# The halved norm between two layers: where its stages, its root and its products lie, and the order of the work around it

## What is computed

```python
h_lat = h_lat + gt_l[:, None, :] * y_lat                 # y_lat = (o * silu(gate)) @ mla_w_out
...
u_lat = rms_norm(h_lat, norm_g[i]) * (1.0 + sc_l[:, None, :]) + sh_l[:, None, :]
proj = u @ w_in                                          # fourier_mix
z, gate = proj[..., :FOURIER_WIDTH], proj[..., FOURIER_WIDTH:]
...
return (y * jax.nn.silu(gate)) @ w_out
```

## Time and profile before

| | us |
|---|---|
| median of 3 runs | 1463.97 |
| lowest and highest | 1463.37, 1466.03 |
| profiled execution, its own time | 1463.78 |
| span of its trace | 1461.9 |
| first-half norm to end of the gate product FG, about | 354 to 397 of the span |

### The profile page before, as it was taken

How to read it: one execution, slowest core, us unless ns; L and a number is a source line. 1 busy time by engine, 2 the same in 40 slices (tenths; PEclk the granted TensorE clock), 3 DMA queues, 4 the chain that set the end, 5 groups by cost and what they waited for, 6 DMA issues and landing times.

```text
span 1461.9 us, 18234 instructions
## 1 busy us (share of the span) xinstructions
PE 1392.6 (95%) x6933; PEld 1152.3 (79%) x6933; DVE 756.2 (52%) x1024; ACT 578.2 (40%) x886; POOL 501.8 (34%) x235
## 2 busy tenths in 40 slices
PE   5899899999899999999999989999999999999998
PEld 2388677778788888877779879878888888888887
DVE  1389788853845536567542443460635435253342
ACT  4233455543533344445643344343334223132231
POOL 1124001135442294411224214214465444444441
PEclk9999999999999999989999889879999999999999
DMA  9686000116231143311222212113333333333322
GB/s 311 195 275 196 20 11 25 30 43 221 72 113 46 43 143 87 101 43 44 61 72 74 59 43 73 56 30 114 92 95 95 94 100 100 90 96 100 100 89 71
DMA packets 204501, 136.18 MB, mean 93 GB/s; under 512 B 7033, under 2 KB 185834, under 8 KB 204442
## 3 DMA queue, kind: packets, MB, share of 16 engines
q1 hardware_dynamic: 204442, 135.37, 30.8%
HBM read 130.64 MB, written 4.72 MB: 93 GB/s over the span
## 4 chain that ended last, share of the span: by engine, by line
PE 81%; DVE 11%; ACT 3%; issue 2%; DMA 1%; SPq 1%; POOL 0%; ACTq 0%; DVEq 0%
PE psum L1868 26%; PE psum L1869 25%; PE psum L1870 25%; DVE neg_max L1410 1%; DMA w_raw<-in_mla_w_in 1%; DVE pt_lo L1403 1%; PE psum L1909 1%; DVE probs L1398 1%; ACT probs L829 1%; PE psum L2262 1%; ACT w_hi L712 1%; DVE u_lo L1498 0%; PE psum L2388 0%; DVE stage L1783 0%; PE psum L1974 0%
## 5 line engine op out<-in xcount | busy, mean ns | idle before, releaser
L602 POOL TENSOR_TENSOR w_lo<-w_raw,w_hi 128x1024 fp32r<-128x1024 f32 x180 | 438.8, 2441 | 770.7 <-ACT w_hi L712 642.8
L1868 PE MATMUL psum<-u_hi,w_hi 128*128 128x512 f32 (+1 forms) x960 | 374.6, 390 | 12.2 <-DVE u_lo L1498 6.3
L1869 PE MATMUL psum<-u_lo,w_hi 128*128 128x512 f32 (+1 forms) x960 | 364.8, 380 | 0.0
L1870 PE MATMUL psum<-u_hi,w_lo 128*128 128x512 f32 (+1 forms) x960 | 364.4, 380 | 0.0
L712 ACT ACTIVATE w_hi<-w_raw 128x1024 fp32r<-128x1024 f32 x180 | 189.2, 1055 | 197.7 <-PE psum L1870 155.7
L1868 PEld LDWEIGHTS psum<-u_hi,w_hi 128*128 128x128 f32 x960 | 184.2, 192 | 52.6 <-issue 8.9
L1870 PEld LDWEIGHTS psum<-u_hi,w_lo 128*128 128x128 f32 x960 | 184.0, 192 | 34.3
L1869 PEld LDWEIGHTS psum<-u_lo,w_hi 128*128 128x128 f32 x960 | 184.4, 192 | 32.9 <-issue 1.7
L1868 PE MATMUL psum<-y_hi,w_hi 128*128 128x512 f32 x416 | 162.4, 390 | 0.0
L1869 PE MATMUL psum<-y_lo,w_hi 128*128 128x512 f32 x416 | 161.9, 389 | 0.0
L1870 PE MATMUL psum<-y_hi,w_lo 128*128 128x512 f32 x416 | 161.8, 389 | 0.0
(11 more groups left out here) (414 smaller groups left out, 2348.0 us busy)
## 6 DMA issues: line engine op xcount, KB each, us to landing
w_raw<-in_w_in SPq DMA_DIRECT2D x52, 512.0 KB, 3.8
w_raw<-in_w_up SPq DMA_DIRECT2D x32, 512.0 KB, 4.0
w_raw<-in_w_down SPq DMA_DIRECT2D x32, 512.0 KB, 3.7
ada_back<-in_w_ada SPq DMA_DIRECT2D x7, 2048.0 KB, 8.6
ada_w<-in_w_ada SPq DMA_DIRECT2D x5, 2048.0 KB, 9.5
w_raw<-in_fno_w_in SPq DMA_DIRECT2D x16, 512.0 KB, 3.9
w_raw<-in_mla_w_in SPq DMA_DIRECT2D x11, 512.0 KB, 8.1
w_raw<-in_mla_w_out SPq DMA_DIRECT2D x8, 512.0 KB, 3.8
```

The costliest lines, as they stand in the source:

```text
L602: pool.tensor_tensor(WL[:, j, :], RAW[:, j % 2, :], f(WH[:, j, :]), ALU.subtract).then_inc(lo_done, 1)
L1868: pe.matmul(out, ah, bh, start=first, stop=False)
L1869: pe.matmul(out, ah, bl, start=False, stop=False)
L1870: return pe.matmul(out, al, bh, start=False, stop=last)
```

## The change

- The first half's stages go to PSUM, three in turn (banks 0 to 2), and its reciprocal root to bank 3 (`norm_stage`, `norm_rstd`). The second half keeps its two stages in SBUF, and its root in `RS`.
- Both sums over partitions go to bank 3. The second one is multiplied after chunk 2 of tile 1 of FG instead of at the end of tile 0.
- FG's first half goes to banks 4 to 7, its second to banks 0 to 3. The SiLU of a gate tile, one instruction over both halves before, becomes two of 256 columns.
- ACT's order: split FG 0 comes before chunk 0; split FG 1, 2 and 3, each with the square before it, come behind chunks 0 to 2, 3 to 5, and 6 and 7 of `half_hi`.
- DVE's order: stage c + 2 is written before `half_lo` of chunk c, and residual chunks 5 and 6 come after `half_lo` 0 and 3 (before: 0 and 4). In the second half the order is as it was, written otherwise.

```diff
--- before.py
+++ after.py
@@ -275,6 +275,14 @@
 
         def bank(b, n=T, o=0):
             return PB[:, b * T + o:b * T + o + n]
+
+        def norm_stage(h, c):
+
+            return E[:, c % 2, HALVES[1]] if h else bank(c % 3, HALF)
+
+        def norm_rstd(h):
+
+            return RS[:, HALVES[1]] if h else bank(3, HALF)
 
         def kv_bank(c):
 
@@ -893,12 +901,12 @@
 
             def half_root(h):
                 act.wait_ge(norm["ss"], h + 1)
-                act.activation(RS[:, HALVES[h]], bank(4 * h, HALF), ACT.Sqrt, scale=1.0 / D, bias=EPST[:]).then_inc(norm["sqrt"], 1)
+                act.activation(RS[:, HALVES[h]], bank(3, HALF), ACT.Sqrt, scale=1.0 / D, bias=EPST[:]).then_inc(norm["sqrt"], 1)
 
             def half_hi(h, c):
                 n = KC * h + c
                 act.wait_ge(norm["e"], n + 1)
-                act.activation(UH[:, c, HALVES[h]], E[:, n % 2, HALVES[h]], ACT.Identity, bias=ADAL[1][:, c:c + 1]).then_inc(norm["hi"], 1)
+                act.activation(UH[:, c, HALVES[h]], norm_stage(h, c), ACT.Identity, bias=ADAL[1][:, c:c + 1]).then_inc(norm["hi"], 1)
 
             def root(n, b):
                 act.wait_ge(norm["ss"], so_far(n, "ss") + 1)
@@ -910,11 +918,13 @@
             for j in range(4):
                 half_square(4 + j, 4 + j, HALVES[0])
             half_root(0)
-            for j in range(4):
+            half_square(8, 4, HALVES[1])
+            split_hi(FG, None, 0)
+            for j, chunks in ((1, (0, 1, 2)), (2, (3, 4, 5)), (3, (6, 7))):
+                for c in chunks:
+                    half_hi(0, c)
                 half_square(8 + j, 4 + j, HALVES[1])
                 split_hi(FG, None, j)
-                for c in {0: (0,), 1: (1, 2, 3, 4), 2: (5, 6, 7)}.get(j, ()):
-                    half_hi(0, c)
             half_root(1)
             for c in range(KC):
                 half_hi(1, c)
@@ -925,8 +935,8 @@
 
             for j in range(4):
                 act.wait_ge(tile_done, FG + j + 1)
-                act.activation(SG[:, j, :].rearrange("p (a n) -> p a n", a=2),
-                               PB[:].rearrange("p (a n) -> p a n", a=2)[:, :, j * T:j * T + HALF], ACT.Silu)
+                act.activation(SG[:, j, HALVES[0]], bank(4 + j, HALF), ACT.Silu)
+                act.activation(SG[:, j, HALVES[1]], bank(j, HALF), ACT.Silu)
                 split_hi(FG + 4, None, j)
             for j in range(4):
                 act.wait_ge(tile_done, FG + 4 + j + 1)
@@ -1482,20 +1492,19 @@
 
             def half_rstd(h):
                 v.wait_ge(norm["sqrt"], h + 1)
-                v.reciprocal(RS[:, HALVES[h]], RS[:, HALVES[h]]).then_inc(norm["rstd"], 1)
+                v.reciprocal(norm_rstd(h), RS[:, HALVES[h]]).then_inc(norm["rstd"], 1)
                 v.wait_ge(norm["rstd"], h + 1)
 
             def half_e(h, c):
-                n = KC * h + c
-                if n >= 2:
-                    v.wait_ge(norm["lo"], n - 1)
-                v.scalar_tensor_tensor(E[:, n % 2, HALVES[h]], HT[:, c, HALVES[h]], MULL[1][:, c:c + 1], RS[:, HALVES[h]],
+                if c >= 3 - h:
+                    v.wait_ge(norm["lo"], KC * h + c - 2 + h)
+                v.scalar_tensor_tensor(norm_stage(h, c), HT[:, c, HALVES[h]], MULL[1][:, c:c + 1], norm_rstd(h),
                                        ALU.mult, ALU.mult).then_inc(norm["e"], 1)
 
             def half_lo(h, c):
                 n = KC * h + c
                 v.wait_ge(norm["hi"], n + 1)
-                v.scalar_tensor_tensor(UL[:, c, HALVES[h]], E[:, n % 2, HALVES[h]], ADAL[1][:, c:c + 1], f(UH[:, c, HALVES[h]]),
+                v.scalar_tensor_tensor(UL[:, c, HALVES[h]], norm_stage(h, c), ADAL[1][:, c:c + 1], f(UH[:, c, HALVES[h]]),
                                        ALU.add, ALU.subtract).then_inc(norm["lo"], 1)
 
             def second_half(c):
@@ -1510,20 +1519,21 @@
                 attention_added(c, bank(c - 4, HALF), HALVES[0])
             second_half(4)
             half_rstd(0)
-            for c in range(KC + 1):
-                if c < KC:
-                    half_e(0, c)
-                if c >= 1:
-                    half_lo(0, c - 1)
-                if c == 1 or c == 5:
-                    second_half(5 if c == 1 else 6)
+            half_e(0, 0)
+            half_e(0, 1)
+            for c in range(KC):
+                if c < KC - 2:
+                    half_e(0, c + 2)
+                half_lo(0, c)
+                if c == 0 or c == 3:
+                    second_half(5 if c == 0 else 6)
             second_half(7)
             half_rstd(1)
-            for c in range(KC + 1):
-                if c < KC:
-                    half_e(1, c)
-                if c >= 1:
-                    half_lo(1, c - 1)
+            half_e(1, 0)
+            for c in range(KC):
+                if c < KC - 1:
+                    half_e(1, c + 1)
+                half_lo(1, c)
 
             v.wait_ge(norm["lo"], 2 * KC)
             for r in range(6, 8):
@@ -2095,25 +2105,25 @@
 
             def half_sums(h):
                 pe.wait_ge(norm["acc"], 2 + 4 + 4 * (h + 1))
-                pe.matmul(bank(4 * h, HALF), ONES[:], ACC[:, HALVES[h]], start=True, stop=True).then_inc(norm["ss"], 1)
-
-            def half_tile(h, j, k0=0, k1=KC, ready=False):
+                pe.matmul(bank(3, HALF), ONES[:], ACC[:, HALVES[h]], start=True, stop=True).then_inc(norm["ss"], 1)
+
+            def half_tile(h, j, b, k0=0, k1=KC, ready=False):
 
                 for k in range(k0, k1):
                     if ready:
                         pe.wait_ge(norm["lo"], KC * h + k + 1)
-                    mm = three(bank(4 * h + j, HALF), wsl(WH, j, k), wsl(WL, j, k), UH[:, k, HALVES[h]], UL[:, k, HALVES[h]],
+                    mm = three(bank(b, HALF), wsl(WH, j, k), wsl(WL, j, k), UH[:, k, HALVES[h]], UL[:, k, HALVES[h]],
                                k == 0, k == KC - 1)
                 return mm
 
             for j in range(4):
                 pe.wait_ge(lo_done, MO + 4 + j + 1)
-                half_tile(0, j).then_inc(mo_half, 1)
-            half_tile(1, 0, 0, 6)
+                half_tile(0, j, j).then_inc(mo_half, 1)
+            half_tile(1, 0, 4, 0, 6)
             half_sums(0)
-            half_tile(1, 0, 6, KC).then_inc(tile_done, 1)
+            half_tile(1, 0, 4, 6, KC).then_inc(tile_done, 1)
             for j in range(1, 4):
-                half_tile(1, j).then_inc(tile_done, 1)
+                half_tile(1, j, 4 + j).then_inc(tile_done, 1)
 
             def sums(n, b):
                 pe.wait_ge(norm["acc"], so_far(n, "acc") + KC + 2)
@@ -2121,11 +2131,14 @@
 
             for j in range(4):
                 pe.wait_ge(lo_done, FG + j + 1)
-                half_tile(0, j, ready=j == 0)
-                if j == 0:
+                if j == 1:
+                    half_tile(0, j, 4 + j, 0, 3)
                     half_sums(1)
+                    half_tile(0, j, 4 + j, 3, KC)
+                else:
+                    half_tile(0, j, 4 + j, ready=j == 0)
             for j in range(4):
-                half_tile(1, j, ready=j == 0).then_inc(tile_done, 1)
+                half_tile(1, j, j, ready=j == 0).then_inc(tile_done, 1)
             for j in range(4):
                 product(FG + 4 + j, j, UH, UL)
             for r in range(6, 8):
```

## The result

The changed kernel takes 1455.66 us (median of 4 runs, 1453.05 to 1455.88) against 1464.24 for the one before (1463.37 to 1466.03), a ratio of 0.9936 with a 95% interval of 0.9919 to 0.9953. The range of the prediction, 1450.6 to 1458.8, holds it; the forecast of 1453.4 was 2.3 us too low. The profiled execution took 1455.69 with a span of 1453.9, 8.0 us less than before.

A forecast was written before the change was run, and what follows sets the result against it. PE (busy 95%) was taken to bound the kernel, with 10.8 us lost to stalls and low clock before and in FG. Less 0.1 and 0.3, the gain is 10.4: 1463.78 - 10.4 = 1453.4 us, range 1450.6 to 1458.8.

The forecast's parts named there:

- The 10.8 us at stake: PE's stalls and low clock between attention output and FG's first half: 378.1 less 367.2, claimed as 10.8 us.
- The holds: Three DVE instructions reading two SBUF tensors, each held over 2 us until a POOL weight split ends: 5.8 us together.
- Rival 1: PSUM operands do not free DVE in FG's first half: gain only 3.4 to 5.4 us, about 1459; chance 0.10.
- PSUM's price of nothing: First-half stages and root in PSUM: DVE's 16 instructions priced at 0.48 us each, no change.
- The bound of 0.27 each: Upper bound on DVE's extra cost per PSUM instruction: stages and root 2.4 us later, about 0.8 at the end.
- rival 3: Writing the eight stages to PSUM is dear: at 3.0 us a chunk, tile 0 ends at 380, kernel 1470; chance 0.03.
- The split of FG 2 as the price of the move: On ACT, FG 2's split waits for its DMA until 362.2 with `u_hi` 6 and 7 behind; covered by 0.5 us.
- The second half late by 0.3: PE waits for the last chunk of the norm's second half, after sum, root and reciprocal: 0.3 us of stall.
- 2 us either way behind FG: Low-clock stretches after 378, whose edges can move when all is 10 us earlier: 2 us allowed either way.
- Rival 2: Sum, root or reciprocal slips 2 us more and PE stands at the second half: 1455 to 1457; chance 0.12.
- Moving the weight splits: ACT's weight splits ahead of the next chunk's `u_hi`, 1.05 us each, counted among the rest of the loss.
- Gate halves hidden: SiLU in halves adds 0.3 us per tile on ACT, hidden before FG 4 with 1.6 us spare; uncovered 1.4 us.

The follow-up runs named there:

- tight: Changed kernel with later FG 2 and 3 splits on ACT, POOL's last addition earlier, second sum behind tile 0, second-half stages and root in PSUM: 1454.74 us.
- psum_old_order: Kernel before with only the memory changed: first-half stages (two) and root in PSUM, with the banks and SiLU halves this needs, engine orders as before: 1459.74 us.
- after_again: The changed kernel in another execution, nothing different: 1455.93 us, against 1465.06 for the kernel before.
- before_again: The kernel before in another execution, nothing different: 1463.76 us.
- sbuf_stages: Changed kernel with all its order, but the first half's three stages and root in SBUF: 1461.67 us.
- psum_sum_moved: Kernel before with first-half stages (two) and root in PSUM, old order except the second sum behind chunk 2 of FG tile 1: 1457.92 us.
- root_sbuf: Changed kernel with the first half's root back in SBUF, its stages still in PSUM: 1458.73 us.
- sum_at_end: Changed kernel with the second sum back at the end of tile 0 of FG: 1454.98 us.
- tight_again: The tight kernel in another execution, nothing different: 1454.48 us, against 1455.93 for the changed kernel beside it.

## Why the prediction was right, and where it was off

- *What bounds it.* Right. The 10.8 us at stake are the section before, 43.1, less 32.3 without a wait; the tight kernel measures 32.1. (As written, 378.1 less 367.2 makes 10.9.)
- *The holds.* Right, with their size: taking them away with nothing else brought 6.1 us, against 5.8 for the three holds. The low clock does not go with the holds alone: in psum_old_order, without any hold, it still fell to 0.5, and only the new order kept it at 1.0. Rival 1 (the hold stays) is out in all of the PSUM runs.
- *PSUM's price of nothing.* Right: stages 0.40 from start to start, reciprocal 1.75, `u_lo` 0.48. The bound of 0.27 each and rival 3 are out. The 62 cycles more for a PSUM source, which the Trainium skill's page "VectorE: DVE Perf Modes" (section on the TRN2 errata) gives, are not in these rows: 0.48 us from PSUM and 0.48 from SBUF. The measurement decides. (The prediction counts 17 such instructions; the reciprocal reads SBUF, so they are 16.)
- *The split of FG 2 as the price of the move.* The place was named, with a cover of 0.5 us; it was mis-sized. The step took the weights of FG 0 as there when ACT asks. In the profiled execution they came 0.94 us later, FG 2 began its split at 9.5 us after the section's start where the working had 8.4, and that cost 1.0 us at chunk 6. In after_again it began at 8.3, as in the working, and cost nothing. ACT waited for FG 0 in 4 of the 14 traces, by 0.25 to 0.94 us, once in the kernel before (0.41 in before_again); why stays open.
- *The second half late by 0.3.* Right: 0.3 at 380.22.
- *FG's end 32.7 after the section's start* (386.5 less 353.8) was forecast. Measured were 33.7 and 32.6. The section's gain was forecast as 10.4 and came out as 9.4 and 10.5.
- *The total.* The profiled execution came out 2.3 us above the forecast: 1.8 by the late start of the section, 1.0 by the wait at chunk 6, less 0.4 behind FG. The forecast had nothing for the stretch ahead of the section. Its 2 us either way behind FG were well sized: from FG to the end of the span the traces of the changed kernel have 1064.6 and 1066.4, and all fourteen lie between 1064.4 and 1066.4. A further part is the base: the profiled execution of before, 1463.78, lies 1.3 to 1.7 us under the later medians, against which the changed kernel is 9.1 us faster.
- *Rival 2, and some luck.* Its price of 1455 to 1457 holds the measured 1455.66, and one of its conditions (`u_hi` 6 late on its DMA) came true. The time alone could not tell it from the forecast; the traces do. Rival 2 has PE stand at the second half, and there PE lost 0.3 us; and in after_again chunk 6 was on time and the kernel took 1455.93 all the same. That the 2.3 us stayed inside the range is in part luck, since the largest part of them, the late start, was not in its working.
- *Moving the weight splits.* Wrong in its weight: the prediction counted the splits ahead of `u_hi` on ACT among the rest of the loss. With the holds gone and three stages there, their old place (33.4) costs at most 0.8 us, against 32.6, and is as good as the new one where that pays its price at FG 2 (33.7).
- *Gate halves hidden.* Right: the halves took 0.39 instead of 0.47, POOL's split of FG 4 ended 1.7 us before PE came, and PE has no gap behind 380.22 up to FG 4.

## What to carry to other kernels

When one VectorE instruction among equals takes four times as long, lay GpSimd's timeline beside it: if both read SBUF, putting one of VectorE's two inputs into PSUM frees it, at no cost in these rows, and every tensor input counts, the root that all chunks share too. Before moving work in a queue behind others, list the DMA that it waits for and what then stands behind it; a cover of half a microsecond was gone in one execution out of two here. Judge a local edit by landmarks in the trace: the section repeats within 0.1 us in the kernel before and the tight one, and within 1.1 in the changed one, where a load came late once, while single runs of one kernel differ by up to 3 us. And take a second trace before you explain the last microsecond: here it showed that a repair had nothing to repair.

## What the runs showed of the hardware

- Two SBUF inputs are what counts, not the destination: a stage that writes PSUM and reads two SBUF tensors was held 2.23 us. The Trainium skill's page "SBUF — State Buffer" (section "Who interferes with whom") says the first half of this: a VectorE instruction with two SBUF inputs contends with a GpSimd instruction that reads SBUF, one with a single SBUF input outside the two-port modes does not. All rows shown here agree. It also names `tensor_scalar` among those that can be held with one input; the changed kernel's trace has one, on a 512-column tile, behind POOL's splits of 384.77 to 390.49:

```profile
380.20 0.49 DVE L1351 TENSOR_SCALAR ada_sum<-ada_back,c_act 128x512 f32<-128x512 f32 x1
...
388.15 2.62 DVE L1351 TENSOR_SCALAR ada_sum<-ada_back,c_act 128x512 f32<-128x512 f32 x1
```

- The hold works both ways, and short ones count: POOL's split took 2.63 us beside the stages of sbuf_stages and 5.72 for two beside the modulations (2.40 each in the changed kernel, where DVE reads PSUM beside it), and a 0.74 us addition held a stage to 0.74.
- The granted clock fell to 0.5 without one long stop: in psum_sum_moved behind waits of 1.44 and 0.29 us. But such waits do not settle it. In root_sbuf PE waited 1.37, 0.56 and 0.54 us within 4 us and the clock stayed at 1.00, as these windows show; sum_at_end had one wait of 1.32 and stayed at 1.00; and a wait of 2.1 us near 308 was followed by a lower clock in after_again and not in before. What decides is not shown.

```profile
368.00:371.00 3.00, 2.07 (x14) 1.87 (x15) 2.63 (x6) 1.97 (x5) 2.65 (x2) 1.00 0.54 163
371.00:374.00 3.00, 2.79 (x22) 2.54 (x21) 0.52 (x1) 1.54 (x3) 2.97 (x3) 1.00 0.28 82
```

- The start of the section differs by 3 us between executions, and by 2.2 us between two of one and the same kernel (tight and tight_again).
